# Expert stage of a one-core MoE decoder step: gate and up run one step ahead of down, three and four weight buffers in place of four and two, the lone block ninth

## The reference

```python
def hier_moe(h, w_rg, b_rg, w_re, b_re, w_e_gate, w_e_up, w_e_down):
    ...
    for gi in range(N_GROUPS):
        a = jnp.einsum('btd,edf->btef', h, w_e_gate[gi])
        u = jnp.einsum('btd,edf->btef', h, w_e_up[gi])
        act = jax.nn.silu(a) * u * combine[..., gi, :, None]
        out = out + jnp.einsum('btef,efd->btd', act, w_e_down[gi])
    return out
```

## Time and profile before

| | |
|---|---|
| median of 3 runs | 1289.91 us (1287.24 to 1292.51) |
| the profiled execution's own time | 1285.31 us |
| its span, first to last instruction | 1283.6 us |
| mean granted TensorE clock | 0.937 of full |
| TensorE matmuls busy | 1132.9 us (88%) |
| moved from and to memory | 226.3 MB, mean 176 GB/s |

### The profile page before, as it was taken

How to read it: one execution, slowest core, us unless ns; L and a number is a source line. 1 busy time by engine, 2 the same in 40 slices (tenths; PEclk the granted TensorE clock), 3 DMA queues, 4 the chain that set the end, 5 groups by cost and what they waited for, 6 DMA issues and landing times.

```text
span 1283.6 us, 14709 instructions
## 1 busy us (share of the span) xinstructions
PE 1132.9 (88%) x5998; PEld 755.9 (59%) x5998; DVE 417.1 (32%) x933; ACT 209.0 (16%) x503; POOL 135.7 (11%) x294
## 2 busy tenths in 40 slices
PE   4899998999999996997899999999964987887766
PEld 2345776777788775884577777774432333333322
DVE  2103404456765492667100001013344111111115
ACT  2100000432421122462010000000110100000001
POOL 3001300002103000141000000000001110111101
PEclk9899998999999997997799999999985988898897
DMA  9977432342303443232861412118255999999765
GB/s 358 288 207 215 155 53 64 66 136 44 70 22 64 100 73 67 61 90 86 260 160 66 66 66 66 66 66 336 90 194 224 412 420 419 419 419 418 280 202 187
DMA packets 95309, 226.30 MB, mean 176 GB/s; under 512 B 23566, under 2 KB 42207, under 8 KB 81006
## 3 DMA queue, kind: packets, MB, share of 16 engines
q1 hardware_dynamic: 83270, 202.70, 47.7%
q10 hardware_dynamic: 6992, 12.91, 3.2%
q0 software_dynamic: 4976, 9.71, 2.0%
HBM read 210.60 MB, written 23.08 MB: 182 GB/s over the span
## 4 chain that ended last, share of the span: by engine, by line
PE 40%; issue 4%; DVE 3%; ACTq 2%; DMA 1%; ACT 1%; POOL 0%; POOLq 0%; DVEq 0%
PE ps L555 17%; PE ps L1970 9%; PE ps L1988 6%; PE ps L1698 4%; PE ps L1960 2%; ACTq L1630 1%; PE ps L2213 1%; PE ps L1718 1%; PE ps L1689 1%; DVE actT L2120 1%; ACTq L1631 0%; PE ps L1977 0%; DVE y_pairs L2229 0%; DMA y_pairs<-pair_scratch 0%; DMA x_gathered<-h_scratch,toks 0%
## 5 line engine op out<-in xcount | busy, mean ns | idle before, releaser
L555 PE MATMUL ps<-hT,w_ring 128*128 128x288 f32 x1792 | 446.3, 409 | 11.9 <-PEq L106 10.0
L555 PEld LDWEIGHTS ps<-hT,w_ring 128*128 128x128 f32 x1792 | 340.6, 192 | 105.4 <-issue 13.5
L1970 PE MATMUL ps<-w_gate_up,xT 128*64 128x512 f32 x528 | 122.0, 601 | 1.5 <-DVE xT L2108 1.5
L1988 PE MATMUL ps<-w_down,actT 128*64 128x512 f32 x264 | 74.5, 701 | 40.3 <-issue 35.8
L1970 PEld LDWEIGHTS ps<-w_gate_up,xT 128*64 128x64 f32 x528 | 42.9, 139 | 77.2 <-issue 77.2
L2116 DVE TENSOR_TENSOR act<-silu_gate,ps 128x256 f32<-128x256 f32 x17 | 7.2, 422 | 212.2 <-ACT silu_gate L1931 212.2
L1988 PEld LDWEIGHTS ps<-w_down,actT 128*64 128x64 f32 x264 | 23.0, 160 | 80.0 <-issue 74.0
L555 PE MATMUL ps<-aT,w_ring 128*128 128x288 f32 x256 | 62.5, 406 | 0.9 <-ACT gate_sig L1641 0.9
L555 PE MATMUL ps<-zzT,w_ring 128*128 128x288 f32 x256 | 62.4, 406 | 0.0
L405 PE MATMUL ps<-w_ring,hT 128*128 128x512 f32 x128 | 58.4, 616 | 2.9 <-DMA w_ring<-w_in 2.9
L555 PEld LDWEIGHTS ps<-aT,w_ring 128*128 128x128 f32 x256 | 48.6, 190 | 14.7 <-issue 1.4
(11 more groups left out here) (406 smaller groups left out, 1227.1 us busy)
## 6 DMA issues: line engine op xcount, KB each, us to landing
w_ring<-w_in SPq DMA_DIRECT2D x16, 2048.0 KB, 13.7
w_gate_up<-w_e_gate SPq DMA_DIRECT2D x32, 1024.0 KB, 20.8
w_gate_up<-w_e_up SPq DMA_DIRECT2D x32, 1024.0 KB, 23.8
w_down<-w_e_down SPq DMA_DIRECT2D x32, 1024.0 KB, 23.3
w_ada_slots<-w_ada SPq DMA_DIRECT2D x10, 2048.0 KB, 9.2
w_ring<-w_ada SPq DMA_DIRECT2D x2, 2048.0 KB, 12.5
w_ring<-w_pa SPq DMA_DIRECT2D x2, 2048.0 KB, 14.5
w_ring<-w_pb SPq DMA_DIRECT2D x2, 2048.0 KB, 7.9
```

Source lines behind the costliest of these rows:

```text
L555: last = nc.tensor.matmul(psum[:, bank + hf, 0:HALF], w[:, c, 128 * q:128 * q + 128], x[:, c, HALF * hf:HALF * hf + HALF], start=c == 0, s ...
L1970: last = te.matmul(psum[side(u), s % 2, :], xT[:, s % 2, c, side(u)], gu[s % GU_BUFS][:, u, :, c, :], start=c == 0, stop=c == KC - 1)
L1988: last = te.matmul(psum[side(u), 4 + hf, :], aT[:, s % 2, c, side(u)], wd[s % WD_BUFS][:, u, c, 512 * hf:512 * hf + 512], start=c == 0, st ...
```

## The change

- Three gate/up buffers and four down buffers; the fourth gate/up buffer's 32 KB per partition become two down buffers of 16 KB. Down buffer 2 lies over x2 and is loaded by the merge program once x2 is stored; down buffer 3 lies over the routing's data and is loaded once the table is ready. Gate/up 3 is no longer preloaded, it waits for gate_up(0).
- TensorE's order is gate_up(s+1), act_transposes(s), x_transposes(s+2), down(s). VectorE and GpSimd follow: xT and gathers are one step further ahead.
- SP's order: wait for gate_up(s+1), issue gate/up s+4; wait for down(s), issue down weights s+4. At its end it waits for gate_up(14) and down(12).
- The lone block is step 8, and pairs 8 to 15 are steps 9 to 16.
- x2 is read back to gate/up buffer 2's place, and `y_pairs` lies over down buffer 1 and gate/up buffer 1.

```diff
@@ -1507,12 +1507,21 @@
+LONE_AT = 8
...
-GU_BUFS, WD_BUFS = 4, 2
+GU_BUFS, WD_BUFS = 3, 4
...
+def block_pair(s):
+
+    if s > LONE or s < LONE_AT:
+        return s
+    return LONE if s == LONE_AT else s - 1
@@ -1540,10 +1549,10 @@
     m.gu = [weights("w_gate_up0", ring + 51200), weights("w_gate_up1", ring + 16384),
-            weights("w_gate_up2", base), weights("w_gate_up3", base + 87232)]
-    m.wd = [rows("w_down0", base + 34816), rows("w_down1", ring)]
-    m.kept_rows = ring + 16384
-    m.y_base = ring + 51200
+            weights("w_gate_up2", base)]
+    m.wd = [rows("w_down0", base + 34816), rows("w_down1", ring), rows("w_down2", base + 103616), rows("w_down3", base + 87232)]
+    m.kept_rows = base
+    m.y_base = ring
@@ -1597,6 +1606,8 @@
         load_gate_up(sp, m, ins, 2, (4, 5))
+        sp.wait_ge(x2st, 16 * NT)
+        load_down(sp, m, ins, 2, (4, 5))
@@ -1858,27 +1869,27 @@
     def sync(sp):
-        sp.wait_ge(m.merged["x2st"], 16 * NT)
         sp.wait_ge(overd, 1)
-        load_gate_up(sp, m, ins, 3, (6, 7))
+        load_down(sp, m, ins, 3, (6, 7))
...
         def run(lo, hi):
-            for s in range(lo - GU_BUFS if lo else 0, hi):
-                g, d = s + GU_BUFS, s + WD_BUFS
+            for s in range(lo - WD_BUFS - 1 if lo else -1, hi):
+                g, d = s + 1 + GU_BUFS, s + WD_BUFS
                 if max(lo, GU_BUFS) <= g < hi:
-                    sp.wait_ge(gmm, s + 1)
+                    sp.wait_ge(gmm, s + 2)
                     load_gate_up(sp, m, ins, g, experts(g))
                 if max(lo, WD_BUFS) <= d < hi:
                     sp.wait_ge(dmm, s + 1)
                     load_down(sp, m, ins, d, experts(d))
-            sp.wait_ge(gmm, hi if lo else hi - 3)
+            sp.wait_ge(gmm, hi if lo else hi - 2)
@@ -1895,22 +1906,22 @@
         def run(lo, hi):
             pool.wait_ge(tabd, 4)
-            gather(lo)
-            gather(lo + 1)
+            for s in range(lo, lo + 3):
+                gather(s)
             for s in range(lo, hi):
-                if s + 2 < hi:
-                    gather(s + 2)
+                if s + 3 < hi:
+                    gather(s + 3)
                 scatter(s)
@@ -1984,18 +1995,21 @@
         def run(lo, hi):
             x_transposes(lo)
+            gate_up(lo)
+            x_transposes(lo + 1)
             for s in range(lo, hi):
-                gate_up(s)
                 if s + 1 < hi:
-                    x_transposes(s + 1)
+                    gate_up(s + 1)
                 act_transposes(s)
+                if s + 2 < hi:
+                    x_transposes(s + 2)
                 down(s)
@@ -2109,6 +2123,7 @@
             x_evacuate(lo)
+            x_evacuate(lo + 1)
...
-                if s + 1 < hi:
-                    x_evacuate(s + 1)
+                if s + 2 < hi:
+                    x_evacuate(s + 2)
```

More of the change, by code:

```diff
@@ L1860, in sync @@
     def sync(sp):
-        sp.wait_ge(m.merged["x2st"], 16 * NT)
         sp.wait_ge(overd, 1)
-        load_gate_up(sp, m, ins, 3, (6, 7))
+        load_down(sp, m, ins, 3, (6, 7))
         def experts(s):
-            if s < NE // 2:
-                return 2 * s, 2 * s + 1
-            at = 2 * (s - NE // 2)
+            pair = block_pair(s)
+            if pair < NE // 2:
+                return 2 * pair, 2 * pair + 1
+            at = 2 * (pair - NE // 2)
             sp.wait_ge(overd, 1)
-            return tuple(sp.value_load(m.over[0:1, at + u:at + u + 1], min_val=0, max_val=NE - 1) for u in range(1 if s == LONE else 2))
+            return tuple(sp.value_load(m.over[0:1, at + u:at + u + 1], min_val=0, max_val=NE - 1) for u in range(1 if pair == LONE else 2))
         def run(lo, hi):
-            for s in range(lo - GU_BUFS if lo else 0, hi):
-                g, d = s + GU_BUFS, s + WD_BUFS
+            for s in range(lo - WD_BUFS - 1 if lo else -1, hi):
+                g, d = s + 1 + GU_BUFS, s + WD_BUFS
                 if max(lo, GU_BUFS) <= g < hi:
-                    sp.wait_ge(gmm, s + 1)
+                    sp.wait_ge(gmm, s + 2)
                     load_gate_up(sp, m, ins, g, experts(g))
@@ L1897, in gather @@
             p.indirect_dma_start(out=xg[:, s % 2, :], out_offset=None, in_=m.h2_dram[:, :],
-                                 in_offset=bass.IndirectOffsetOnAxis(ap=m.toks[:, s:s + 1], axis=0),
+                                 in_offset=bass.IndirectOffsetOnAxis(ap=m.toks[:, block_pair(s):block_pair(s) + 1], axis=0),
                                  bounds_check=last_tok, oob_is_err=False).then_inc(gth[s % 2], 16)
@@ L1902, in scatter @@
             pool.wait_ge(yev, s + 1)
-            p.indirect_dma_start(out=m.y_dram[:, :], out_offset=bass.IndirectOffsetOnAxis(ap=m.pairs[:, s:s + 1], axis=0),
+            p.indirect_dma_start(out=m.y_dram[:, :], out_offset=bass.IndirectOffsetOnAxis(ap=m.pairs[:, block_pair(s):block_pair(s) + 1], axis=0),
                                  in_=yo[:, s % 2, :], in_offset=None,
@@ L1968, in gate_up @@
             for c in range(KC):
-                for u in range(1 if s == LONE else 2):
+                for u in range(1 if s == LONE_AT else 2):
                     last = te.matmul(psum[side(u), s % 2, :], xT[:, s % 2, c, side(u)], gu[s % GU_BUFS][:, u, :, c, :],
```

## The result

The changed kernel takes 1279.95 us (median of 9 runs, 1276.53 to 1286.65) against 1289.91 us for the kernel before (9 runs). The ratio is 0.9936, with a 95% interval of 0.9915 to 0.9956. So it is faster by 8.3 us (5.7 to 11.0) by the ratio, and by 10.0 us from median to median. The time is inside the range forecast, but the gain is only half to three fifths of the 16.3 us that the sum gave. The time is also just that of the first rival (about 1280 us), but not by its mechanism, as the end of this document says.

What follows compares the result with a forecast made beforehand. The weight stream bounds the kernel until about 1203 us, then held-back down loads and TensorE's last steps; 18.4 - 1.1 - 1 = 16.3 us off the 1289.9 us median gives about 1273 us, range 1266 to 1282 us.

Steps and rivals of the forecast that it cites:

- the 16.3 us that the sum gave: Whole gain: last down at 1224.0 instead of 1242.4 us, 18.4 us, less 1.1 for cold matmuls and 1 for the scatter.
- the first rival: Tail: scatter behind reload (6.6 us), or cold gate_up(16) with stream 3 us late; gain 8 to 11 us; chance 0.18.
- the last down loads were held back: Near 1203 us: with two down buffers, loads of steps 15 and 16 wait for down(13) and down(14); the stream runs dry.
- The stream's end by bytes: Weight stream's end moves from 1203 to 1211.5 us by bytes over rate, so gate/up 16 has landed at 1206.5 us.
- The opening: First steps from 993.3 us: 0 us of starving, upper bound 3 us; the thin place is gate/up 4.
- The tail of 18.6 us: From last gate/up landing to last copy: gate_up, act transposes, two downs, copy, silu and product, with the surcharge of 1.1.
- the surcharge of 1.1: gate_up(16) behind TensorE's wait may run cold, 2.0 or 2.4 us more; taken once with even odds, 1.1 us.
- The last scatter, 1 us: At the end: the last scatter meets the reload of x2 and the vectors; 1 us lost, bounds 0 and 6.6.
- The lone block "costs and gives nothing": Lone block in the middle: same TensorE time, 3.15 MB of stream saved there and paid at the end; worth nothing.
- The order "worth nothing until the end": Engines' new order saves TensorE some 0.5 us a step where it is not the bound; worth nothing until the end.
- The clock rival: TensorE at the low clock becomes the bound from a gate_up of 11.3 us on; slower, 1304 us; chance 0.05.
- The forecast against the median: Runs' median stands 4.6 us above the profiled execution; 16.3 us taken off 1289.9 gives 1273.6, say 1273 us.

Runs made afterwards that it cites:

- the first deal: The changed kernel with a block's rows dealt evenly over its 64 slots (slot 4*(r mod 16) + r div 16): 1276.77 us, ratio 0.9905.
- the second deal: The changed kernel with a block's rows dealt the other, uneven way (slot 8*(r mod 8) + r div 8): 1287.23 us, ratio 0.998.
- the one without gathered rows: The changed kernel with the gathers' bound set to row 0, so next to no rows move and tokens are left out: 1266.33 us in one execution.

## Why the prediction was right or wrong

- **What bounds the kernel, and that the last down loads were held back: right.** With the old buffers the stage was 255.0 us, with the new ones alone 248.1 us, as short as with the whole change. The stream ran at 416 GB/s from 1000 to 1200 us and had no hole.
- **The stream's end by bytes: right for the mean engine, wrong as a landing.** This is the step that failed. "So gate/up 16 has landed at 1206.5 us" took the sum of bytes over the total rate as the time at which a load is complete. The bytes had passed when the sum said (222.3 us behind the first gate_up against 222.4), but the load was complete only 6.3 us later, with the slowest of 16 engines. Runs with even and uneven deals moved the landing by -3.0 and +6.8 us with the same bytes. With the even deal 3.3 us of the 6.3 remain; their cause stays open, with an estimate in the last section. The profile before already held the clue: in the earlier trace rows the rate does not fall off a cliff at 1203 us, it is at 286 GB/s from 1200 to 1203.5 us. I read that as the end of the bytes. With two down buffers the lateness of the last gate/up load was hidden: it was complete at 1204.3 us, and its gate_up began at 1229.8 us, behind TensorE's backlog. The change took that cover away.
- **The opening.** It measured a little worse than forecast: the first gate_up took 9.70 us (9.24), the second waited 1.41 us for xT, as no act transposes stand between any more, and 1000 to 1020 us ran at 387 GB/s. That is 1.4 us of stream (20 x 30 / 417), inside the bound of 3 us. That the bytes still passed on time is partly luck: the stream then ran at 419 GB/s and not 417, and the 1 us that the sum kept for more gathers and scatters was not needed (7.18 MB against 7.17 before).
- **The tail of 18.6 us: 20.0.** Three small terms: gate_up(16) was warm (7.09, so the surcharge of 1.1 was not due there), the copy to actT was not covered by x transposes, which the last step lacks (0.95 instead of 0.36), and down(16) ran cold behind the copy, silu and product (5.35 instead of 3.65; the granted clock was 0.64 from 1232.5 to 1236 us). The surcharge was real, at another place.
- **The last scatter, 1 us: right.** It landed in 3.21 us; from the last copy to the first load of `y_pairs` it took 5.7 us instead of 4.9. The reload had no other effect that the runs show.
- **The first rival, "about 1280 us": its number came, its mechanism did not.** It put the loss on a scatter behind the reload (0.8 us measured), a cold gate_up(16) (it was warm) and a starved stream (the bytes were on time). The missing time lay in the spread of the landing, which no rival named.
- **The lone block "costs and gives nothing": wrong, as far as the stages tell.** Placed last it costs 2.1 to 4.2 us of stage, because TensorE pays a full step for half the bytes, exactly where TensorE and not the stream is late.
- **The order "worth nothing until the end": right, and at the end it was worth less than nothing.** I counted the copy of down(15) into the tail and did not ask what the old order would give there.
- **The clock rival: right in kind, harmless.** Six of the nine gate_ups behind a wait for weights, those with waits of 2.6 to 4.8 us, took 8.8 to 9.9 us; the other three, the last one behind 2.50 us among them, took 7.1. And gate_up's busy time went from 122.0 to 134.1 us over all steps. It stayed under the 11.3 us from which it would decide.
- **The forecast against the median.** Adding the 4.6 us by which the profiled run lay below the median was borne out: the first gate_up of that run (984.05 us) started earlier than in every later profile.

## What to carry to other kernels

A stream's bytes over its rate gave the mean engine's end here, while a load was complete only with the slowest. Before pricing a load that will stand on the critical path, look at the spread of its landing, and at uneven traffic (a gather of a half-filled block) that shares the engines. Of a change with three parts, price each at the end of the stage by itself: here the buffers carried the gain, the lone block helped a little, and the new order of TensorE (gate and up one step ahead of down), which had nothing to hide while the stream was late, made the last step longer (20.0 us from landing to copy against 15.7).

## What the hardware showed that I had not expected

- Over 200 us of full stream the reports of one down load spread from 4.8 to 17.8 us, and most of that growth came from how the rows of gathers and scatters fall on the sixteen DMA engines: dealing the same rows over other partitions gave spreads of 8.9 and 26.1 us.
- Even the best deal left 7.4 to 8.9 us against 4 to 5 us at the start of the stage. With 34 rows of 64, and every eighth group of four partitions to an engine, two engines of eight still get a row more than the others. One row of 4 KB in each of the 29 gathers and scatters up to the landing, at 26 GB/s for one engine (417 / 16), is 4.6 us, which would be that rest. That is an estimate from these rows and was not tried.
- A down product behind a chain of short waits (1.85 and 0.52 us, one pair of transposes between) took 5.35 us in some kernels (the change, the first deal) and 3.65 us in others (the second deal, the one without gathered rows). What decides between the two was not tested.
